# A decoder step with a routed expert layer: routing table, first weight load, block boundary and row sum changed

## The reference, cut to what matters

```python
x = x + mix @ w_out
x = x + hier_moe(rms_norm(x, norm2_g), ...)

def hier_moe(h, wg, bg, we, be, w_gate, w_up, w_down):
    g_logits = hf @ wg + bg                       # 4 groups, the best one is taken
    p_group  = softmax(g_logits) at the best group
    e_in     = (hf @ we + be) of that group       # 4 experts, the best two are taken
    gate     = softmax(top_2(e_in)) * p_group     # two shares per token
    for e in range(16):
        he = silu(hf @ w_gate[e]) * (hf @ w_up[e])        # 1024 -> 512
        y  = y + combine[:, e] * (he @ w_down[e])         # 512 -> 1024
```

## Time and profile before

| | |
|---|---|
| median of the runs | 1527.43 us |
| time of the profiled execution | 1524.12 us |
| its span, first to last instruction | 1522.3 us |
| TensorE busy | 1215.8 us (80%) |
| VectorE busy | 580.4 us (38%) |
| ScalarE busy | 279.1 us (18%) |
| GpSimd busy | 166.4 us (11%) |
| DMA, mean over the span | 163 GB/s |

### The profile page before, as it was taken

The page is one execution under the profiler, slowest core; times in us unless marked ns, Lnnn a source line. Parts: engine busy times, 40 slices in busy tenths (PEclk is TensorE's granted clock), DMA queues, the critical chain, the costliest instruction groups (busy, mean ns, idle before and its releaser), DMA issues. The chain is left out here.

```text
span 1522.3 us, 16758 instructions
## 1 busy us (share of the span) xinstructions
PE 1215.8 (80%) x6035; PEld 829.9 (55%) x6035; DVE 580.4 (38%) x1045; ACT 279.1 (18%) x529; POOL 166.4 (11%) x197
## 2 busy tenths in 40 slices
PE   0899996893665888888869971299999999999970
PEld 0689995881442656665569971144444444444430
DVE  0730898577775554445342343011011101101106
ACT  3212211326213322233231120000000000000000
POOL 3012321106001000000000002200000000000004
PEclk9999997995865786778889985599999999999995
DMA  5302321101002455433150024548888988888728
GB/s 139 87 15 84 97 97 56 59 0 54 1 17 62 136 160 153 122 108 101 56 198 29 29 83 149 215 174 362 322 317 327 361 315 318 356 333 315 295 104 327
DMA packets 99297, 248.63 MB, mean 163 GB/s; under 512 B 19131, under 2 KB 76864, under 8 KB 90764
## 3 DMA queue, kind: packets, MB, share of 16 engines
q1 hardware_dynamic: 83740, 199.51, 36.0%
q0 software_dynamic: 9664, 32.49, 6.1%
q10 hardware_dynamic: 5824, 15.73, 2.7%
HBM read 217.26 MB, written 30.73 MB: 163 GB/s over the span
## 5 line engine op out<-in xcount | busy, mean ns | idle before, releaser
L1932 PE MATMUL ps<-wg,hgT 128*128 128x512 f32 x352 | 157.8, 602 | 3.1 <-DVE hgT L1887 3.1
L1949 PE MATMUL ps<-mixT,heT 128*128 128x512 f32 x352 | 156.2, 597 | 3.1 <-ACT heT L1855 3.1
L1932 PE MATMUL ps<-wu,hgT 128*128 128x512 f32 x352 | 154.7, 592 | 0.0
L1893 DVE TENSOR_TENSOR he<-sg,ps 128x512 f32<-128x512 f32 x22 | 15.1, 688 | 305.0 <-ACT sg L1851 305.0
L195 PE MATMUL ps<-hT_hi,wz_hi 128*128 128x352 f32 x384 | 127.5, 332 | 0.0
L195 PE MATMUL ps<-hT_lo,wz_hi 128*128 128x352 f32 x384 | 124.3, 324 | 0.0
L195 PE MATMUL ps<-hT_hi,wz_lo 128*128 128x352 f32 x384 | 124.2, 323 | 0.0
L1932 PEld LDWEIGHTS ps<-wg,hgT 128*128 128x128 f32 x352 | 67.8, 193 | 88.9 <-issue 85.2
L1932 PEld LDWEIGHTS ps<-wu,hgT 128*128 128x128 f32 x352 | 66.9, 190 | 84.2 <-issue 84.2
L1949 PEld LDWEIGHTS ps<-mixT,heT 128*128 128x128 f32 x352 | 65.1, 190 | 78.5 <-issue 75.8
L195 PE MATMUL ps<-wo_hi,mix_hi 128*128 128x256 f32 (+1 forms) x288 | 82.7, 287 | 12.1 <-DVE mix_lo L1545 12.1
(11 more groups left out here) (390 smaller groups left out, 1877.3 us busy)
## 6 DMA issues: line engine op xcount, KB each, us to landing
wg<-in_exp_w_gate SPq DMA_DIRECT2D x22, 2048.0 KB, 12.1
wu<-in_exp_w_up SPq DMA_DIRECT2D x22, 2048.0 KB, 16.6
mixT<-in_exp_w_down SPq DMA_DIRECT2D x22, 2048.0 KB, 8.2
kpg<-in_cache_k SPq DMA_DIRECT2D x128, 128.0 KB, 2.0
vpg<-in_cache_v SPq DMA_DIRECT2D x128, 128.0 KB, 2.4
slot_rows<-yo ACTq DMA_DIRECT2D x22, 512.0 KB, 10.5
wz<-in_w_in SPq DMA_DIRECT2D x16, 512.0 KB, 4.1
slot_rows<-Z POOLq DMA_DIRECT2D x14, 512.0 KB, 2.9
```

Of the source, the lines that this page charges most:

```text
L1893: e.tensor_tensor(he[:, b, :], sg[:, b, :], ps[:, 2 * b + 1, :], ALU.mult).then_inc(he_done, 1)
L1932: i = e.matmul(ps[:, 2 * b + n, :], hgT[:, b, k, :], w[:, b, k, :], start=(k == 0), stop=(k == KC - 1))
L1949: i = e.matmul(ps[:, 6 + n, :], heT[:, b, k, :], wd[:, b, k, n * 512:(n + 1) * 512], start=(k == 0), stop=(k == KE - 1))
```

## The change

`route` and `experts` become one block, `mixture`, with no meeting of the engines between them. In it:

- SyncE issues the weights of expert 0 as its first act, without waiting for `tile_exp`. The rule for a tile's expert count is changed so that each expert has at least one tile, so tile 0 is always expert 0.
- The counts are summed by one scan over 144 values with restarts; the number of tiles per expert comes from an integer shift. `prio` is made at the start of the program, `valid` is gone (the counting products run over 128 and over 32 rows instead).
- The table is made on chip: from one-hots of a pair's tile (`in_tile`, `entry`) and of its row (`in_row`) 18 products on TensorE sum, into PSUM, token number and share for each slot. A slot that no pair fills gets a row number beyond the last token. VectorE turns the sums into `table` in SBUF. The expert of each tile follows after the table.
- The rows of x go from `x2` to a DRAM tensor `acc` ("sum_rows") during `out_projection`, by SyncE. A tile's result is scaled by its slots' shares as it leaves PSUM, and GpSimd adds it to `acc` by an indirect DMA that accumulates. Each of these waits for the one before it.
- `combine` goes. At the end, `finish` copies `acc` to the outputs, DRAM to DRAM, on two queues.
- The 14 zeroing DMAs become 2.

```diff
@@ projections, gpsimd
-                    if 5 <= i < 5 + SLOT_TILES - 2 * LEAST_PAIRS:
-                        t = 2 * LEAST_PAIRS + i - 5
-                        e.dma_start(m.yd[t * P:(t + 1) * P, :], zrow).then_inc(m.s_zero_rows, 16)
+                        for to in (m.h2d, m.acc):
+                            e.dma_start(to[TOK:TOK + P, :], zrow).then_inc(m.s_zero_rows, 16)
@@ out_projection, sync
+                for t in range(NT):
+                    e.wait_ge(x2_done, NT * (NQ - 1) + t + 1)
+                    e.dma_start(m.acc[t * P:t * P + rows_of(t), :], m.x2[0:rows_of(t), t, :]).then_inc(acc_set, 16)
+                e.wait_ge(acc_set, 16 * NT)
@@ mixture, sync
+                load(0, 0, slice(0, 1), True)
                 e.wait_ge(tiles_known, 1)
+                load(1, 1, expert(1), True)
+                e.wait_ge(plan, 1)
+                with e.Fori(1, pairs(e)) as j:
+                    load(2 * j, 0, expert(2 * j))
+                    load(2 * j + 1, 1, expert(2 * j + 1))
@@ mixture, gpsimd
+                def next_share(s, b):
+                    e.tensor_copy(scol[b][:], m.table[:, ds(s, 1), 1])
+                    e.drain().then_inc(s_ready, 1)
+                def scatter(s, b, before, last=False):
+                    e.wait_ge(y_a, s + 1)
+                    e.wait_ge(y_v, s + 1)
+                    if before is not None:
+                        e.wait_ge(y_sent[1 - b], 16 * before)
+                    e.tensor_copy(dcol[b][:], m.table[:, ds(s, 1), 0])
+                    e.drain()
+                    e.indirect_dma_start(out=m.acc, out_offset=bass.IndirectOffsetOnAxis(ap=dcol[b][:, 0:1], axis=0),
+                                         in_=yo[:, b, :], in_offset=None, compute_op=ALU.add).then_inc(y_sent[b], 16)
+                    if not last:
+                        next_share(s + 1, 1 - b)
...
+                with e.Fori(1, n - 2) as j:
+                    gather(2 * j + 4, 0)
+                    scatter(2 * j, 0, j)
+                    gather(2 * j + 5, 1)
+                    scatter(2 * j + 1, 1, j + 1)
...
@@ mixture, scalar (vector: the same wait, and the scale on its half)
-                    e.copy(yo[:, b, 0:512], ps[:, 6, :]).then_inc(y_a, 1)
-                    e.wait_ge(y_a, s + 1)
-                    e.wait_ge(y_v, s + 1)
-                    e.dma_start(m.yd[ds(s * P, P), :], yo[:, b, :]).then_inc(y_sent[b], 16)
+                    e.wait_ge(s_ready, s + 1)
+                    e.activation(yo[:, b, 0:512], ps[:, 6, :], ACT.Copy, scale=share[b]).then_inc(y_a, 1)
@@ mixture, vector
-                for t in range(NT):
-                    e.tensor_tensor(run[:, t + 1, :], run[:, t, :], ps[:, 1, t * NE:(t + 1) * NE], ALU.add)
...
-                for j in range(NT):
-                    e.scalar_tensor_tensor(out=ntile[:], in0=run[:, NT, :], scalar=float(P * j), ...)
...
+                e.tensor_tensor_scan(run[:], m.restart[:]..., count_ps, 0.0, ALU.mult, ALU.add)
+                e.tensor_scalar(filled[:], run[:]...[:, :, NT - 1], float(P - 1), float(P), ALU.add, ALU.max)
+                e.tensor_scalar(ntile_i[:], filled[:], 7, None, ALU.logical_shift_right)
...
+                e.tensor_tensor(in_tile[:], m.lane[:, 0:S]..., where[:, 1]..., ALU.is_equal)
+                e.tensor_tensor(entry[:, :, :, 0, :], in_tile[:], m.tok1[:]..., ALU.mult)
+                e.tensor_tensor(entry[:, :, :, 1, :], in_tile[:], gate[:]..., ALU.mult)
+                for t in range(NT):
+                    e.tensor_tensor(in_row[:, t], m.lane[:]..., where[:, 0, :, t]..., ALU.is_equal).then_inc(hot, 1)
...
+                e.scalar_tensor_tensor(out=m.table[:, :, 0], in0=rows_ps[:, 0:S], scalar=-1.0, in1=spare[:],
+                                       op0=ALU.add, op1=ALU.add).then_inc(table_ready, 1)
@@ mixture, tensor
+                for t in range(NT):
+                    e.wait_ge(hot, t + 1)
+                    r = rows_of(t)
+                    for c in range(2):
+                        i = e.matmul(rows_ps, in_row[0:r, t, c, :], entry[0:r, c, t].rearrange("p a s -> p (a s)"),
+                                     start=(t == c == 0), stop=(t == NT - 1 and c == 1))
@@ finish
+                e.dma_start(m.y_prompt[0, 0:HALF, :], m.acc[0:HALF, :]).then_inc(sent, 16)
+                e.dma_start(m.y_sample.rearrange("b l d -> (b l) d"), m.acc[SEQ:TOK, :]).then_inc(sent, 16)
+                e.wait_ge(sent, 48)
+            @block.scalar
+                e.dma_start(m.y_prompt[0, HALF:SEQ, :], m.acc[HALF:SEQ, :]).then_inc(sent, 16)
```

More of the change, by code:

```diff
@@ new lines, in mixture @@
+        where_i, where = sb("where_i", [P, 2, 2, NT], I32), sb("where", [P, 2, 2, NT])
+        in_tile, entry, in_row = sb("in_tile", H4), sb("entry", [P, 2, NT, 2, S]), sb("in_row", [P, NT, 2, P])
+        spare = sb("spare", [P, S])
+        te, tsum = sb("te", [1, S, NE]), sb("tsum", [1, S])
+        gdiff, exps, oh_done, cnt_mm, hot, rows_mm, table_ready, tiles_known, plan = (
+            sem("r_" + n) for n in ("gdiff", "exps", "oh", "cnt_mm", "hot", "rows_mm", "table", "tiles", "plan"))
@@ new lines, in mixture @@
+        hg, hgT = sb("hg", [P, 2, D]), sb("hgT", [P, 2, KC, P])
+        gcol, dcol, scol = ([sb(f"{n}{i}", [P, 1], I32) for i in range(2)] for n in ("gcol", "dcol", "scol"))
+        share = [c[:].bitcast(F32) for c in scol]
+        sg, he, heT = sb("sg", [P, 2, DE]), sb("he", [P, 2, DE]), sb("heT", [P, 2, KE, P])
+        yo = sb("yo", [P, 2, D])
+        pair = lambda n: [sem(f"{n}{i}") for i in range(2)]
+        gu_in, dn_in, hg_in, y_sent = m.gu_in, m.dn_in, pair("hg_in"), pair("y_sent")
@@ L1666, in _, with act_silu, step @@
             @block.scalar
             def _(e):
+                def act_silu(s, b):
+                    e.wait_ge(gu_mm, s + 1)
+                    e.activation(sg[:, b, :], ps[:, 2 * b, :], ACT.Silu).then_inc(silu, 1)
+                def step(s, b, j, last=False):
+                    e.wait_ge(he_mm, s + 1)
+                    e.copy(heT[:, b], ps[:, 2 * b, :].rearrange("p (k t) -> p k t", k=KE)).then_inc(he_out, 1)
+                    e.wait_ge(d_mm, s + 1)
+                    if not (isinstance(j, int) and j == 0):
+                        e.wait_ge(y_sent[b], 16 * j)
+                    e.wait_ge(s_ready, s + 1)
+                    e.activation(yo[:, b, 0:512], ps[:, 6, :], ACT.Copy, scale=share[b]).then_inc(y_a, 1)
+                    if not last:
+                        act_silu(s + 2, b)
@@ new lines, in _ @@
+                e.drain()
+                e.scalar_tensor_tensor(out=slot[:], in0=base[:].unsqueeze(1).broadcast_to(B3), scalar=float(P), in1=slot[:],
+                                       op0=ALU.mult, op1=ALU.add)
+                e.drain()
+                e.tensor_tensor(pick2[:], oh[:], slot[:].unsqueeze(1).broadcast_to([P, 2, NT, NE]), ALU.mult)
+                e.drain()
+                e.tensor_reduce(sf[:], pick2[:], AX.X, ALU.add)
+                e.drain()
+                e.tensor_copy(slots[:], sf[:])
@@ new lines, in _ @@
+                e.drain()
+                e.tensor_scalar(where_i[:, 0], slots[:], P - 1, None, ALU.bitwise_and)
+                e.tensor_scalar(where_i[:, 1], slots[:], 7, None, ALU.logical_shift_right)
+                e.drain()
+                e.tensor_copy(where[:], where_i[:])
+                e.drain()
+                e.tensor_tensor(in_tile[:], m.lane[:, 0:S].unsqueeze(1).unsqueeze(1).broadcast_to(H4),
+                                where[:, 1].unsqueeze(3).broadcast_to(H4), ALU.is_equal)
@@ new lines, in _ @@
+                e.drain()
+                e.tensor_tensor(entry[:, :, :, 0, :], in_tile[:], m.tok1[:].unsqueeze(1).unsqueeze(3).broadcast_to(H4), ALU.mult)
+                e.tensor_tensor(entry[:, :, :, 1, :], in_tile[:], gate[:].unsqueeze(3).broadcast_to(H4), ALU.mult)
+                for t in range(NT):
+                    e.tensor_tensor(in_row[:, t], m.lane[:].unsqueeze(1).broadcast_to([P, 2, P]),
+                                    where[:, 0, :, t].unsqueeze(2).broadcast_to([P, 2, P]), ALU.is_equal).then_inc(hot, 1)
@@ L1918, in _ @@
             def _(e):
+                e.wait_ge(oh_done, 1)
+                full, rest = slice(0, NT - 1), NT - 1
+                for out, lhsT in ((rank_ps, m.back), (count_ps, m.ones)):
+                    to = out.rearrange("p (n t) -> p n t", t=NT)
+                    e.matmul(to[:, :, full], lhsT[:], both[:, :, full], start=True, stop=True)
+                    i = e.matmul(to[:, :, rest], lhsT[0:NS, :], both[0:NS, :, rest], start=True, stop=True)
+                i.then_inc(cnt_mm, 1)
+                for t in range(NT):
[4 more added lines that the diff above has]
+                                     start=(t == c == 0), stop=(t == NT - 1 and c == 1))
+                i.then_inc(rows_mm, 1)
                 def turn(s, b, j):
@@ L1943, in step @@
                     e.wait_ge(dn_in[b], 16 * j + 16)
```

(4 more changed lines are left out.)

332 lines of the change are left out of this document (120 added, 212 removed).

## The result

The changed kernel takes 1477.45 us, the median of 4 runs (1466.94 to 1478.46); the kernel before, run beside it, 1528.39 us (4 runs, 1525.73 to 1529.83). The ratio is 0.965, with a 95% interval of 0.961 to 0.970. Forecast were 1471 us, in a range of 1456 to 1500: direction and range hold, and the saving is 51 us instead of 56.5. The profiled execution took 1478.46 us, its span is 1476.7 us.

What follows compares the result with a forecast made beforehand. TensorE bounds the loop; routing with GpSimd's DMAs through DRAM bounds the start, the row sum the end. Gains 31 + 0 + 25.5 = 56.5 us off 1527.43 give 1471 us, range 1456 to 1500.

Steps and rivals of the forecast that it cites:

- The bound: Expert stage start: VectorE's routing, then GpSimd's DMAs through DRAM; tile loop: TensorE; end: row sum, 46.5 us without TensorE work.
- The start: Last logits to first gate product: on-chip table and earlier gather bring the gate to 950.8 from 981.87, gain 31 us.
- The four counting products: TensorE in the routing: from 926.3 to about 928.1, each pair's added short second instruction some 0.2 us.
- the table's 36 pieces: TensorE's 18 table products, two instructions each: 0.17 to 0.2 us a piece, 6.1 to 7.2 us, taken as 6.5.
- The late gather: Start: first gather falls behind the second tile's weights, landing 11.5 us instead of 4.3, time 1478; chance 11%.
- Code late: Routing chain: instruction fetch waits behind the 6 MB of early weights, 11.5 us, time 1482; chance 5%.
- The loop: Tile loop: accumulating scatter lands in 10.5 to 17 us, hidden; steps stay at 22.15 us, gain 0.
- the rival spoke of: Loop: the add doubles the scatter's landing to 21 us beside the weights, costing 28 us, time 1499; chance 10%.
- The end: After the last down product: scatter, meeting and final copies finish at T + 21, gain 25.5 us.
- The copies: Final DRAM to DRAM copy: 4.33 MB at 416 GB/s in 10.4 us, plus 2.4 issue and landing, 0.4 second issue.
- The bytes don't count twice: Denied rival, final copy: each byte counts twice, read and written, 10.4 us more, time 1481; chance 14%.
- its first rival: Start: first gather falls behind the second tile's weights, 11.5 us instead of 4.3, time 1478; chance 11%.

Runs made afterwards that it cites:

- e2: The kernel before, with only expert 0's weights issued early, as the routing starts: 1525.40 us, ratio 1.000 to the kernel before.
- e5: The changed kernel with the old nine adds and nine compares on VectorE instead of scan and shift: 1478.57 us, ratio 0.968 to the kernel before.
- e6: The changed kernel plus 17 unused products keeping TensorE busy in the routing: 1465.78 us, ratio 0.960 to the kernel before.
- e1: The changed kernel with expert 0's weights issued only after the list of tile experts: 1481.11 us, ratio 0.972 to the kernel before.
- e3: The changed kernel with routing and tiles as two blocks again, early weights kept: 1483.44 us, ratio 0.972 to the kernel before.
- e4: The changed kernel with a plain overwriting scatter instead of the adding one, so outputs lack the sum: 1472.99 us, ratio 0.966 to the kernel before.
- e9: The changed kernel run once more, unedited: 1475.80 us, ratio 0.966 to the kernel before.

## Why the prediction held, and where it was off

- **The bound, right.** Scatters and the way through DRAM ended last at the start, the row sum at the end. e2 shows the other side: the weights alone, without the scatters' removal, move nothing. No run puts the scatters back into the changed kernel, so the table's share is read from rows: the first gather is issued 27.2 us behind the logits instead of 48.3, 21.1 us sooner (3.3 of them the counts', by e5), and the other 6.6 us are its shorter landing.
- **The start, 27.65 instead of 31.** The order of events is the forecast one, each a little late. Two rows were too cheap. The four counting products took 2.6 us (931.14 to 933.73) instead of 1.8: the second piece of each pair, for 32 rows, takes 0.3 us, not 0.1. And the table's 36 pieces took 8.13 us, 0.226 each, where I had taken 6.5 and 7.2 as the upper bound: this is the largest miss of the stage, 1.6 us, and it lies outside its bounds. Two slips made it. The line through 20 and 144 columns gives 0.21 us at 64, not 0.17 to 0.2. And the row of 20 columns mixes 16 pieces with weights of 128 columns and 16, of the last tile, with weights of 32. The same product of the tile before, with weights of 128 columns throughout, took 0.215 us a piece; so at this clock small pieces hardly get cheaper with fewer columns. Whether the loading of their weights sets the pace, no run shows. Copy and drain ahead of the first gather, 1.4 instead of 1.0, and a landing of 4.65 instead of 4.3 make the rest; VectorE's chain, 7.1 us from counts to the first `in_row` used against 6.85, was nearly right. e6 shows what the low clock costs: 1.0 us in the counting products, 3.8 in the table's, 0.8 in the transposes, and 3.0 in the first gate.
- **The late gather, a rival that didn't come but stood close.** The gather kept 0.93 us of the 1.5 us of lead. With 0.23 us of lead (e1) and 0.29 us behind (e3) its rows came after 11.4 and 11.8 us. The single block pays by this. The early weights pay by this too, but not by this alone: without them the up weights landed only 0.9 us ahead of the late gate (e1).
- **Code late: no sign.** From `gmax` to `both` VectorE took 6.38 us in both kernels, though now beside 6 MB of weights; the stall that this rival spoke of doesn't show on that chain, nor in e2.
- **The loop, right.** 493.22 against 493.94; the landing of 12.9 us lies in the 10.5 to 17 that were taken, and a step stays at 22.15. e4 shows that the add is 1.4 us of it. The Trainium skill (Collectives: The Full Stack, "The bandwidth ceiling: the fold count and why AG ≠ RS ≠ AR") says that a reduce-scatter between cores ran at half of an all-gather's rate, since its add reads two sources. Where nothing else moves e4 comes near it, 6.1 against 3.3 us; beside the weights, the place that the rival spoke of, it is 12.9 against 11.5.
- **The end, 22.0 instead of 25.5.** The issue at T + 2.0 (1.9) was right. The last landing with the meeting took 6.6 us (6.0), since the landing without other traffic was read from a gather, which has no add. The copies took 15.9 us instead of 13.1, and the term that fails is the transfer, 4.33 MB at 416 GB/s in 10.4 us. The DMA engines were busy for 13 us at a share of 0.98, where 11 at a share of 1 were forecast, and moved 331 GB/s meanwhile. The 416 came from a row of gathers and stores between DRAM and SBUF, which holds no copy from DRAM to DRAM and so couldn't price one. The bytes don't count twice; that rival would have made it 23.5.
- **Ahead of the routing, +4.76, no part of the miss.** It is this execution's more than the change's (e9). By the medians the saving is 50.9 us, in e9 50.2, and the three stages behind the logits give 27.65 + 0.72 + 22.0 = 50.4 alone. So the 6.5 us by which the time lies above 1471 are nearly all the start's 3.4 and the end's 3.5, less 0.7 in the loop. The two went the same way, and nothing but the loop's 0.7 hid a part of them. But the number alone would not have told the forecast from its first rival, which stood at 1478; the first gather's 4.65 us do.

The terms together: 4.76 - 27.65 - 0.72 - 22.0 = -45.6, the difference of the spans.

## What to carry to other kernels

When a chain of small steps moves to TensorE, price its products at the clock that the engine has there, from rows with weights of the same size, and see what a few products without use would give back: here 17 of them gave back 8.8 us, and nothing needed their results. A small gather issued at about the same moment as a large load can wait for most of it, and a meeting of engines can undo its lead. For a term worked out from a bandwidth, take the rate from a transfer of the same kind, here DRAM to DRAM; and cut two profiles into stages before putting a few us down to an edit.

## What the runs showed of the hardware

- A gather of 512 KB issued within 0.31 us of megabytes of weights, ahead of them or behind, landed after 11.2 to 11.8 us; issued 0.93 us ahead, its rows were there after 4.65 us. Where between 0.23 and 0.93 us the change lies, no run shows.
- An indirect DMA that adds holds GpSimd 1.58 us at its issue instead of 0.98. It landed in 6.1 us instead of 3.3 at its shortest, and in 12.9 instead of 11.5 beside the weights.
- A scatter whose rows mostly are out of bounds can follow one that writes them for little: with both the end came 7.3 us after the first one's issue.
- TensorE's granted clock, 0.5 in the routing of the changed kernel, was 1.0 through 28 us of routing in which added products kept the engine busy 24.4 us; a piece of 64 columns then took 0.12 us instead of 0.226.
- Two copies and a third of 128 KB, 4.33 MB from DRAM to DRAM, kept the DMA engines at a share of 0.98 for 13 us and moved 331 GB/s; gathers and stores between DRAM and SBUF moved 416 at a share of 1.02.
